# Turning x raw, scaling by channel before and by token after the products, and keeping the turned x as the residual

## The chip, the cores and the metric

The kernel runs on one core of one Trainium2 chip. A core has a matrix engine (TensorE, PE in the profile; its weight loads are PEld), a vector engine (VectorE, DVE), a scalar engine (ScalarE, ACT), a general one (GpSimd, POOL), and a queue engine (SyncE, SP) which issues most transfers. Transfers run on 16 DMA engines. Each engine works through its own list of instructions in order, and waits on semaphores. The metric is the device time of one execution in microseconds (us).

## The reference, cut to what matters

One layer of a hybrid decoder over 1024 prompt tokens and 8 x 4 sample tokens (T = 1056), 1024 channels. The part that the change touches:

```python
def rmsnorm(x, g):
    y = x * lax.rsqrt(jnp.mean(x * x, axis=-1, keepdims=True) + EPS)
    return y * g

z = rmsnorm(x, g_mix) @ w_in          # 1024 -> 5648 columns, cut into
# mLSTM q, k, v, output gate; mi, mf (4 each); FoX q, k, v (8 heads x 64); ff (8); ga, gb (1024 each)
m_ig, m_lf = mi + b_mi, log_sigmoid(mf + b_mf)
f_lf       = log_sigmoid(ff + b_ff)
y_m = mlstm(...)                      # 4 heads of 128, chunks of 128, with a state
y_f = softmax(q k^T + F[t] - F[s]) v  # FoX: 8 heads, F = cumsum(f_lf); samples over a paged cache
hm  = rmsnorm(y_m, g_mh) * sigmoid(mo)
x   = x + (sigmoid(ga) * (hm @ w_pa) + sigmoid(gb) * (y_f @ w_pb)) @ w_out
gu  = rmsnorm(x, g_ffn) @ w_gu;  x = x + (silu(gu[:F]) * gu[F:]) @ w_down     # F = 2816
x   = x + sigmoid(rmsnorm(x, g_ple) @ w_ple_gate) * (p @ w_ple_proj)
```

The factor of rmsnorm is a product of a token factor (1/sqrt of the mean square) and a channel factor (g_mix).

## The kernel before, in words

All products are in fp32 of a reduced format, in three passes: an operand is split into a high part (made by ACT) and a low part (the difference, made by DVE or POOL), and high x high, high x low and low x high are summed. The order of every engine's work is written out by hand, and there are five phases; at the end of each, all five engines wait for one another (`end_phase`, `begin_phase`).

Phase 1 (0 to 228.7 us) normalises x, turns it, and makes the first 27 units of z. A token tile of 128 rows (the ninth has the 32 sample rows) is loaded by SP, squared and summed on ACT, scaled on DVE (`norm`), turned by 8 transposes on PE (L2034), copied as the high part `acth` by ACT (L1129), and DVE makes the low part `actl` (L1547). Then PE makes the small gates mi, mf, ff for all tokens (L2050), and 27 units, each one token tile by 512 columns in 24 matmuls (L2066); the weights come in pieces of 128 x 1024 (`wraw`), of which ACT makes the high part (L1146) and POOL the low part (L927). ACT evacuates a unit to `stage` (L1153) and SP stores it to a DRAM scratch. DVE and ACT turn the gates into the running sums that later phases need; PE turns those into columns (L2072), and starts phase 2's units with `f_unit(0)` (L2089).

Phase 2 (to 447.1) has the mLSTM heads and the other 27 units.

Phase 3 (to 866.8) has the 8 FoX heads. Beside them PE makes 60 gate units, 20 blocks c = u//3 of 128 gate channels by 1056 tokens (mo, ga, gb), half a unit at a time between the steps of a head (L2220). Weights for a block: load `fraw` (`load_gate`, L744), high part on ACT (L1271), low part on POOL (`split_gate`, L988). ACT evacuates a unit to `fout` (L1278), and SP stores a block (`store_gate`, L748). A head g needs the row `nF` of its negated running sums on all partitions (`load_row`, L738), which DVE adds to the logits (L1719); `nb` (L1723) is what frees a logits bank and is awaited by PE's later logits (L2177). The head's output is divided on DVE (`yb`, L1737) and stored by SP (`store_y`, L752) when the next head is under way; DVE overwrites `yb` only after that. SP's list in phase 3 is this:

```python
for g in range(HF):
    for u in range(PRE + 7 * g if g else 0, PRE + 7 * g + 7):
        if u % 3 == 2:
            store_gate(u // 3)
            if u // 3 + 3 < NGATE // 3: load_gate(u // 3 + 3)
        if u == PRE + 7 * g + 4 and g: store_y(g - 1)
    if g < HF - 1: load_row(g + 1)
```

POOL's list has, for head g, the low part of the values (`low_values`, L984), the splits for u from PRE + 7g - 2 to PRE + 7g + 4, and the scaling of the next head's q and k (`norm_head`). PRE is 4.

Phase 4 (to 978.9) has the sample attention, in two groups of 4 sequences: keys (`keys4`, turning pages at L2286), logits, and values (`values4`, L2342). Between group 0's logits and values PE turns raw x, loaded again by SP, into `XR`, the residual with channels on partitions; `load_values(0)` (L811) waits until x is turned, since the pages lie where x was.

Phase 5 merges the branches, adds into XR, and makes the FFN and the last gate (L2396 are its matmuls). Its gate blocks are loaded from scratch (`gs`) and passed through a sigmoid on ACT (L1433), and DVE multiplies a product by them (L1914).

Of the kernel before, what the change touches and what calls it, by code (L numbers as in the profile page):

```python
# [14 lines left out]
F32 = mybir.dt.float32  # L15
# [7 lines left out]
P = 128  # L23
# [11 lines left out]
W = 512  # L35
# [19 lines left out]
def program(nc, a, o):  # L55

    ctx = ExitStack()
    with ctx:
# [42 lines left out]
        ptb = take("ptb", [1, DB * PAGES], I32)  # L101
        attn_consts_end = top[0]
# [15 lines left out]
        xt = take("xt", [P, 2, D])  # L118
        xn = take("xn", [P, 2, D])
        gmix = take("gmix", [P, D])  # L120
        ssq = take("ssq", [P, 4])
        wg = take("wg", [P, KC, GW])
        wgh = take("wgh", [P, KC, GW], F32R)
        wgl = take("wgl", [P, KC, GW], F32R)
        p1_small = top[0]
        top[0] = rows_base
        gx = take("gx", [GW, T])
# [9 lines left out]
        top[0] = max(top[0], p1_small)  # L137
        gbias = take("gbias", [GW, 1])
# [4 lines left out]
        ms_row = take("ms_row", [HM, T])  # L143
        assert top[0] <= ring_end
# [61 lines left out]
        nF = take("nF", [P, SEQ])  # L206
        qst = take("qst", [P, SEQ], F32R)
# [22 lines left out]
        xr4 = at("xr4", top[0] - GB * PAGES * W * 4, [P, NCH, D])  # L230
# [19 lines left out]
        xs4 = at("xs4", scr4, [NS, D])  # L250
# [106 lines left out]
        x_in = [sem("x_in0"), sem("x_in1")]  # L357
        small_in = sem("small_in")
        ssum_done = sem("ssum_done")
        sq_done = sem("sq_done")  # L360
        xn_done = sem("xn_done")
        xt_done = sem("xt_done")
        xhi_done = sem("xhi_done")
        xlo_done = sem("xlo_done")
        dve_own = sem("dve_own")
# [46 lines left out]
        gmh_in = sem("gmh_in")  # L412
        ecol_set = sem("ecol_set")
# [27 lines left out]
        nF_in = sem("nF_in")  # L441
        sq3 = sem("sq3")
# [50 lines left out]
        x4_in = [sem(f"x4_in{i}") for i in range(3)]  # L493
        x4_mm = sem("x4_mm")
        x4_a = sem("x4_a")
        x4_d = sem("x4_d")


# [11 lines left out]
        gv_in = again("gv_in")  # L510
        y5_in = [again("y5_in0"), again("y5_in1")]
# [78 lines left out]

        def zA_at(q, i):
            return zA_rows[q * T + i * P:q * T + i * P + trows(i), :]
# [10 lines left out]
        def _(sp):  # L603

            sp.dma_start(gmix[:], a["g_mix"][0].partition_broadcast(P)).then_inc(small_in, 16)
            sp.dma_start(ptb[:], a["page_table"].rearrange("b n -> (b n)").unsqueeze(0)).then_inc(pt_in, 16)
            sp.wait_ge(consts, 1)
            sp.dma_start(gbias[0:HM, :], a["b_mi"].rearrange("a h -> h a"), allow_slow_non_contiguous=True).then_inc(small_in, 16)
# [3 lines left out]
            w_v = a["w_in"][0].rearrange("(k p) n -> p k n", p=P)  # L612
            for c, n, src in ((0, HM, OFF_MI), (32, HM, OFF_MI + HM), (64, HF, OFF_FF)):
                sp.dma_start(wg[:, :, c:c + n], w_v[:, :, src:src + n], allow_slow_non_contiguous=True).then_inc(wg_in, 16)
            with sp.Fori(0, NCH // 2) as g:
                for s in range(2):
                    row = sp.snap(g * 256 + s * P)
                    sp.wait_ge(xn_done, 2 * g + s + 1)
                    sp.dma_start(xt[:, s], a["x_prompt"][0][bass.ds(row, P), :]).then_inc(x_in[s], 16)
            sp.wait_ge(xn_done, NCH + 1)  # L620
            sp.dma_start(xt[0:NS, 0], a["x_sample"].rearrange("b s d -> (b s) d")).then_inc(x_in[0], 16)

            def load_group(q):
                c = group_columns(q)
                for j in range(PIECES):
                    sp.wait_ge(w_lo1, q * PIECES + j + 1)
                    sp.dma_start(wraw[:, j], w_v[:, 2 * j:2 * j + 2, c:c + W]).then_inc(w_in1[j], 16)

            def store_units(q):
                for i in range(XTILES):  # L630
                    u = q * XTILES + i
# [1906 lines left out]
```

## Time and profile before

| what | value |
|---|---|
| median of 3 runs | 2133.38 us (2132.53 to 2136.48) |
| the profiled execution | 2136.39 us, of which the span is 2134.7 |
| PE, PEld busy | 91%, 85% of the span |
| DVE, ACT, POOL busy | 38%, 25%, 30% |
| mean granted clock of PE | 0.954 of full speed |
| phases end at | 228.7, 447.1, 866.8, 978.9, 2134.7 us |

The time is the device time of an execution; the span is what the profiler saw from its first to its last instruction. Shares of busy time are averages over the five phases, which have different limits: PE was busy 185.4 of phase 1's 228.7 us, 386.4 of phase 3's 419.7, and 64.2 of phase 4's 112.1.

### The profile page before, as it was taken

The page shows a single profiled execution, that of the slowest core. Times are in us where ns is not written, and L with a number is a line of the kernel's source. Part 1 is how long each engine was busy: PE and PEld are TensorE (multiplying, and loading weights), DVE is VectorE, ACT ScalarE, POOL GpSimd, SP SyncE. Part 2 cuts the span into 40 slices and gives each one's busy share as a digit, 9 for nine tenths or more (in the row PEclk, how much of TensorE's full clock was granted, in tenths as well). Part 3 has the DMA queues.
Part 4 walks back from the last instruction along what each step waited for, and adds up shares of the span by engine and source line. Part 5 has one row for each costly group of instructions (what it writes and reads, how often), then busy time and mean ns, then how long its engine had stood idle before and what let it go on. Part 6 is the DMA issues. An engine that isn't in the chain of part 4 may idle for free.

```text
span 2134.7 us, 31432 instructions
## 1 busy us (share of the span) xinstructions
PE 1936.5 (91%) x12117; PEld 1811.3 (85%) x12117; DVE 818.2 (38%) x1486; ACT 542.5 (25%) x930; POOL 642.6 (30%) x473
## 2 busy tenths in 40 slices
PE   2999999979998989465979899999999999999898
PEld 2777788868998989444979899999999999998798
DVE  4500233226655655422563232233323332235333
ACT  5311234224444543112322211001100011003311
POOL 0414223032222222002225634334333434335121
PEclk8999999989999999777999899999999999999899
DMA  4222543153323231565321211111111111120111
GB/s 126 70 87 83 172 158 117 67 156 98 95 76 99 76 95 41 181 237 209 106 90 49 69 40 39 43 55 49 49 39 39 59 39 39 41 83 25 36 56 41
DMA packets 203277, 177.78 MB, mean 83 GB/s; under 512 B 49046, under 2 KB 168058, under 8 KB 203162
## 3 DMA queue, kind: packets, MB, share of 16 engines
q1 hardware_dynamic: 156890, 159.92, 23.6%
q10 hardware_dynamic: 45280, 16.58, 3.2%
q8 instruction: 57, 0.93, 0.2%
q0 software_dynamic: 1024, 0.13, 0.1%
q14 instruction: 26, 0.21, 0.0%
HBM read 139.52 MB, written 39.24 MB: 84 GB/s over the span
## 4 chain that ended last, share of the span: by engine, by line
PE 81%; DVE 7%; issue 3%; ACT 3%; DMA 2%; SPq 2%; POOL 1%; ACTq 0%; DVEq 0%; POOLq 0%
PE pair L2396 26%; PE bank L2396 21%; PE bank L2089 7%; PE bank L2220 7%; PE bank L2066 5%; PE pair L2204 3%; PE pair L2066 2%; PE pair L2188 1%; PE pair L2286 1%; DMA scratch_yT<-yb 1%; DVE yb L1737 1%; PE pair L2177 1%; PE pair L2166 1%; SPq L796 1%; PE pair L2050 1%
## 5 line engine op out<-in xcount | busy, mean ns | idle before, releaser
L2396 PE MATMUL bank<-acth,wha 128*128 128x352 f32 x640 | 212.4, 332 | 31.6 <-DVE actl L1889 16.8
L2396 PE MATMUL bank<-actl,wha 128*128 128x352 f32 x640 | 209.6, 328 | 0.0
L2396 PE MATMUL bank<-acth,wla 128*128 128x352 f32 x640 | 209.1, 327 | 0.0
L2220 PE MATMUL bank<-acth,fwh 128*128 128x352 f32 x480 | 162.0, 337 | 15.5 <-POOL fwl L988 15.5
L2396 PE MATMUL pair<-hh,whb 128*128 128x352 f32 x528 | 171.1, 324 | 0.2 <-DVE XR L1994 0.2
L2396 PE MATMUL pair<-hl,whb 128*128 128x352 f32 x528 | 169.2, 320 | 0.0
L2396 PE MATMUL pair<-hh,wlb 128*128 128x352 f32 x528 | 169.0, 320 | 0.0
L1994 DVE TENSOR_TENSOR XR<-XR,pair 128x352 f32<-128x352 f32 x264 | 135.1, 518 | 86.0 <-PE pair L2396 84.8
L1070 POOL TENSOR_TENSOR hl<-un,hh 128x352 fp32r<-128x352 f32 x66 | 62.3, 944 | 342.6 <-ACT hh L1486 342.6
L2220 PE MATMUL bank<-acth,fwl 128*128 128x352 f32 x480 | 155.6, 324 | 0.0
L2220 PE MATMUL bank<-actl,fwh 128*128 128x352 f32 x480 | 155.1, 323 | 0.0
L2396 PEld LDWEIGHTS bank<-acth,wha 128*128 128x128 f32 x640 | 124.0, 194 | 33.8 <-DVE actl L1889 17.0
L1027 POOL CAST wha<-raw 128x1024 fp32r<-128x1024 f32 x46 | 48.9, 1064 | 329.7 <-PE pair L2396 139.8
L2089 PE MATMUL bank<-ring,acth 128*128 128x512 f32 (+1 forms) x432 | 136.6, 397 | 0.3 <-issue 0.3
L1486 ACT CAST hh<-un 128x352 fp32r<-128x352 f32 x66 | 32.2, 487 | 397.3 <-DVE un L1979 397.3
L2396 PEld LDWEIGHTS bank<-actl,wha 128*128 128x128 f32 x640 | 124.2, 194 | 0.0
L2396 PEld LDWEIGHTS bank<-acth,wla 128*128 128x128 f32 x640 | 123.8, 193 | 0.0
L1029 POOL TENSOR_TENSOR wla<-raw,wha 128x1024 fp32r<-128x1024 f32 x46 | 112.7, 2450 | 3.7
L2396 PE MATMUL pair<-acth,whb 128*128 128x352 f32 x352 | 113.5, 322 | 0.0
L2396 PE MATMUL pair<-actl,whb 128*128 128x352 f32 x352 | 112.7, 320 | 0.0
L2396 PE MATMUL pair<-acth,wlb 128*128 128x352 f32 x352 | 112.7, 320 | 0.0
L1029 POOL TENSOR_TENSOR wlb<-raw,whb 128x1024 fp32r<-128x1024 f32 x44 | 105.6, 2399 | 3.5
(442 smaller groups left out, 4803.5 us busy)
## 6 DMA issues: line engine op xcount, KB each, us to landing
raw<-in_w_gu SPq DMA_DIRECT2D x44, 512.0 KB, 3.8
wraw<-in_w_in SPq DMA_DIRECT2D x24, 512.0 KB, 5.8
scratch_zA<-stage SPq DMA_DIRECT2D x48, 256.0 KB, 2.0
raw<-in_w_down SPq DMA_DIRECT2D x22, 512.0 KB, 3.6
scratch_zT<-fout SPq DMA_DIRECT2D x20, 528.0 KB, 3.1
fraw<-in_w_in SPq DMA_DIRECT2D x20, 512.0 KB, 4.9
gs<-scratch_zT SPq DMA_DIRECT2D x16, 528.0 KB, 3.5
kpg<-in_cache_k SPq DMA_DIRECT2D x32, 256.0 KB, 5.2
```

Of the source, the lines that this page charges most:

```text
L796: return [sp.value_load(ptb[0:1, n:n + 1], min_val=0, max_val=NPOOL - 1) for n in range(g * GB * PAGES, (g + 1) * GB * PAGES)]
L1027: nc.gpsimd.tensor_copy(hi, raw[:, j]).then_inc(pool_own, 1)
L1029: nc.gpsimd.tensor_tensor(lo, raw[:, j], hi.bitcast(F32), ALU.subtract).then_inc(w_split, 1)
L1070: nc.gpsimd.tensor_tensor(hl[:, j, t * TW:(t + 1) * TW], un[:, (3 * j + t) % 2, :], hh[:, j, t * TW:(t + 1) * TW].bitcast(F32), ALU.subtra ...
L1486: nc.scalar.copy(hh[:, j, t * TW:(t + 1) * TW], un[:, v % 2, :]).then_inc(h_hi, 1)
L1737: own.step(nc.vector.reciprocal(y, pC[DH:, m * 256:(m + 1) * 256]))
L1994: nc.vector.tensor_tensor(x, x, BANK[4 + u % 4][:, 0:TW], ALU.add).then_inc(x6_done, 1)
L2066: ins = nc.tensor.matmul(BANK[u % 3][0:rows, :], x[:, k, i * P:i * P + rows], w, start=n == 0, stop=n == 3 * KC - 1)
L2089: ins = nc.tensor.matmul(BANK[u % 2][0:rows, :], x[:, k, i * P:i * P + rows], w, start=n == 0, stop=n == 3 * KC - 1)
L2204: ins = nc.tensor.matmul(pC[:, m * 256 + skip:(m + 1) * 256], v[:, j, :], x[:, base + j * 256 + skip:base + (j + 1) * 256], start=n == 0, ...
L2220: ins = nc.tensor.matmul(BANK[u % 2][:, 0:TW], w[:, c % 2, k, :], x[:, k, t * TW:(t + 1) * TW], start=n == 0, stop=n == 3 * KC - 1)
L2396: ins = nc.tensor.matmul(out, w[i](k), x[j](k), start=n == 0, stop=n == total - 1)
```

## The change

- Phase 1: x is not normalised ahead. A tile is turned raw; DVE multiplies it by g_mix, a factor per partition now (`tile_scaled`, from `gcol`), which gives `tf`; ACT copies the raw turned tile for a store to a scratch `xT`, and makes the high part of `tf`; DVE makes the low part. The squares are summed meanwhile, and the token factor `rstd` comes in two lots. The unit of a tile follows its turn, and ACT multiplies by `rstd` as it evacuates a unit, here and in phase 2. The small gates come behind the first nine units; for them, `rstd` is put in a row on all partitions (`rvB`) by 9 matmuls with diagonals. x and the first weights are first in SP's list.
- Phase 3: that row, stored and loaded as `rv3`, multiplies each gate block in `fout` on POOL (`scale_gate`, a multiply of 128 x 1056), and `store_gate` waits for this.
- Phase 4: the loads, transposes and copies of x go, with their waits.
- Phase 5: SP loads `XR` from `xT` in 9 transfers behind `hst5`, 4.33 MB, and DVE waits for them before w_out's loop.

```diff
+            load_tile(0)
+            load_piece0(0, 0)
+            load_piece0(0, 1)
+            load_tile(1)
+            load_piece0(0, 2)
+            load_piece0(0, 3)
+            load_tile(2)
             sp.dma_start(ptb[:], a["page_table"].rearrange("b n -> (b n)").unsqueeze(0)).then_inc(pt_in, 16)
             sp.wait_ge(consts, 1)
+            for c, n, src in ((0, HM, OFF_MI), (32, HM, OFF_MI + HM), (64, HF, OFF_FF)):
+                sp.dma_start(wg[:, :, c:c + n], w_v[:, :, src:src + n], allow_slow_non_contiguous=True).then_inc(wg_in, 16)
+            for i in range(XTILES):
+                store_tile(i)
+                if i + 3 < XTILES:
+                    load_tile(i + 3)
+                if 2 <= i < 6:
+                    load_piece0(1, i - 2)
+                if i >= 3:
+                    store_unit(i - 3)
...
+            sp.dma_start(RS[2 * HM:2 * HM + 1, :], rvB[0:1, :]).then_inc(rows_out, 16)
...
             def store_gate(c):
-                sp.wait_ge(f_out, 3 * c + 3)
+                sp.wait_ge(f_rv, c + 1)
                 sp.dma_start(o["zT"][c * P:(c + 1) * P, :], fout[:, c % 2, :]).then_inc(f_st[c % 2], 16)
...
             load_row(0)
+            sp.dma_start(rv3[:], o["rows"][2 * HM:2 * HM + 1, :].partition_broadcast(P).rearrange("p a t -> p (a t)")).then_inc(g_in, 16)
             sp.dma_start(gqk[:, 0, :], a["g_qn"][0].partition_broadcast(P)).then_inc(g_in, 16)
...
             def load_values(g, pages):
-                sp.wait_ge(x4_mm, XTILES)
                 if g:
                     sp.wait_ge(o4_mm, g)
...
             pages = load_pages(0)
             load_keys(0, pages)
-            sp.wait_ge(ms4, 1)
-            sp.dma_start(xs4[:], a["x_sample"].rearrange("b s d -> (b s) d")).then_inc(x4_in[0], 16)
-            for i in range(2):
-                sp.dma_start(xr4[:, 4 * i:4 * i + 4, :], a["x_prompt"][0][512 * i:512 * i + 512, :].rearrange("(i p) d -> p i d", p=P)).then_inc(x4_in[1 + i], 16)
             load_values(0, pages)
...
             sp.dma_start(hst5[:], o["hT"].rearrange("(c p) t -> p c t", p=P)).then_inc(h5_in, 16)
+            for i in range(XTILES):
+                sp.dma_start(XR[:, :, token_cols(i)], xT_at(i)).then_inc(xr_in, 16)
             for c in range(2, KC):
                 if c % 2 == 0 and c < 6:
...
+            def scale_gate(c):
+                pool.wait_ge(f_out, 3 * c + 3)
+                nc.gpsimd.tensor_tensor(fout[:, c % 2, :], fout[:, c % 2, :], rv3[:], ALU.mult).then_inc(f_rv, 1)
+
             def split_gate(c):
                 pool.wait_ge(f_hi, c + 1)
                 nc.gpsimd.tensor_tensor(fwl[:, c % 2], fraw[:, c % 2], fwh[:, c % 2].bitcast(F32), ALU.subtract).then_inc(f_lo, 1)
...
             pool.wait_ge(g_done, 1)
+            pool.wait_ge(g_in, 48)
             norm_head(0)
             for g in range(HF):
                 low_values(g)
                 for u in range(PRE + 7 * g - 2 if g else 0, PRE + 7 * g + 5):
-                    if u % 3 == 2 and u // 3 + 2 < NGATE // 3:
-                        split_gate(u // 3 + 2)
+                    if u % 3 == 2:
+                        if u // 3 + 2 < NGATE // 3:
+                            split_gate(u // 3 + 2)
+                        scale_gate(u // 3)
                 if g < HF - 1:
                     norm_head(g + 1)
+            for u in range(PRE + 7 * HF - 2, NGATE):
+                if u % 3 == 2:
+                    scale_gate(u // 3)
             end_phase(pool)
 
...
+            def tile_out(i):
+                act.wait_ge(tf_done, i + 1)
+                if i >= 2:
+                    act.wait_ge(xs_st[i % 2], 16 * (i // 2))
+                nc.scalar.copy(xs[:, i % 2, :, 0:trows(i)], turn_pair(i)).then_inc(xs_done, 1)
+                nc.scalar.copy(acth[:, :, token_cols(i)], tf[:, i % 2, :, 0:trows(i)]).then_inc(xhi_done, 1)
...
+                if u == 0 or u == 4:
+                    act.wait_ge(rs_done, u // 4 + 1)
+                nc.scalar.mul(stage[0:rows, u % 3], unit_bank(u)[0:rows, :], rstd[0:rows, u % XTILES:u % XTILES + 1]).then_inc(unit_out, 1)
...
-                nc.scalar.copy(stage[0:rows, u % 3], BANK[u % 2][0:rows, :]).then_inc(fu_out, 1)
+                i = u % XTILES
+                nc.scalar.mul(stage[0:rows, u % 3], BANK[u % 2][0:rows, :], rstd[0:rows, i:i + 1]).then_inc(fu_out, 1)
...
+            def tile_scaled(i):
+                if i == 0:
+                    dve.wait_ge(g_col, 16)
+                dve.wait_ge(xt_done, i + 1)
+                if i >= 2:
+                    dve.wait_ge(xlo_done, i - 1)
+                nc.vector.tensor_tensor(tf[:, i % 2, :, 0:trows(i)], turn_pair(i), gcol[:].unsqueeze(2).to_broadcast([P, KC, trows(i)]),
+                                        ALU.mult).then_inc(tf_done, 1)
+
+            def tile_low(i):
+                dve.wait_ge(xhi_done, i + 1)
+                nc.vector.tensor_tensor(actl[:, :, token_cols(i)], tf[:, i % 2, :, 0:trows(i)], acth[:, :, token_cols(i)].bitcast(F32),
+                                        ALU.subtract).then_inc(xlo_done, 1)
...
+                nc.vector.reciprocal(rstd[:, first:last], ssq[:, first:last]).then_inc(rs_done, 1)
+
+            tile_scaled(0)
+            for i in range(1, XTILES):
+                if i == 3:
+                    recips(0, 0, 4)
+                if i == 7:
+                    recips(1, 4, XTILES)
+                tile_scaled(i)
+                tile_low(i - 1)
+            tile_low(NCH)
+            dve.wait_ge(rs_done, 2)
+            dve.wait_ge(xlo_done, XTILES)
+            for i in range(XTILES):
+                n = trows(i)
+                ins = nc.vector.tensor_scalar(dg[0:n, i, 0:n], ident[0:n, 0:n], rstd[0:n, i:i + 1], None, ALU.mult)
+            ins.then_inc(dg_done, 1)
             dve.wait_ge(gate_mm, 1)
+            nc.vector.tensor_copy(rvB[:, 0:512], BANK[5][:])
+            nc.vector.tensor_copy(rvB[:, 512:SEQ], BANK[7][:])
+            nc.vector.tensor_copy(rvB[:, SEQ:], BANK[4][:, 0:NS]).then_inc(dg_done, 1)
+            dve.wait_ge(dg_done, 2)
...
             for t in range(NT):
-                ins = nc.vector.tensor_scalar(gx[:, t * TW:(t + 1) * TW], BANK[5 + t][0:GW, 0:TW], gbias[:, 0:1], None, ALU.add)
+                cols = slice(t * TW, (t + 1) * TW)
+                own.step(nc.vector.tensor_tensor(gx[:, cols], BANK[2 + t][0:GW, 0:TW], rvB[0:GW, cols], ALU.mult))
+                ins = nc.vector.tensor_scalar(gx[:, cols], gx[:, cols], gbias[:, 0:1], None, ALU.add)
             ins.then_inc(gate_x, 1)
+            dve.wait_ge(gate_x, 1)
             dve.wait_ge(gate_l, 1)
...
+            dve.wait_ge(xr_in, 16 * XTILES)
...
+            def turn_tile(i):
+                pe.wait_ge(x_in[i % 3], 16 * (i // 3) + 16)
+                if i >= 2:
+                    pe.wait_ge(xs_done, i - 1)
+                n = trows(i)
                 for k in range(KC):
-                    ins = nc.tensor.transpose(BANK[2 * s + k // 4][:, (k % 4) * P:(k % 4) * P + rows],
-                                              xn[0:rows, s, k * P:(k + 1) * P], ident[0:rows, 0:rows])
+                    ins = nc.tensor.transpose(PAIR[i % 2][:, k * P:k * P + n], xt[0:n, i % 3, k * P:(k + 1) * P], ident[0:n, 0:n])
                 ins.then_inc(xt_done, 1)
...
+            turn_tile(0)
+            turn_tile(1)
+            for i in range(XTILES):
+                if i + 2 < XTILES:
+                    turn_tile(i + 2)
+                unit(i)
+
+            pe.wait_ge(dg_done, 1)
+            for i in range(XTILES):
+                n = trows(i)
+                out = BANK[5 + i // 4 * 2][:, i % 4 * P:(i % 4 + 1) * P] if i < NCH else BANK[4][:, 0:NS]
+                ins = nc.tensor.matmul(out, ones[0:n, :], dg[0:n, i, 0:n], start=True, stop=True)
+            ins.then_inc(gate_mm, 1)
+            pe.wait_ge(wg_lo, 1)
+            for t in range(NT):
+                n = 0
...
+                if t == 2:
+                    pe.wait_ge(dg_done, 2)
...
             pe.wait_ge(unit_out, MG * XTILES)
+            pe.wait_ge(col_done, 1)
             f_unit(0)
...
-            for n in range(XTILES):
-                i = (n - 1) % XTILES
-                if n in (0, 1, 5):
-                    pe.wait_ge(x4_in[(n + 3) // 4], 16)
-                if n >= 2:
-                    pe.wait_ge((x4_a, x4_d)[n % 2], n // 2)
-                for k in range(KC):
-                    x = xr4[:, i, k * P:(k + 1) * P] if i < NCH else xs4[:, k * P:(k + 1) * P]
-                    ins = nc.tensor.transpose((pA, pB)[n % 2][:, k * P:k * P + trows(i)], x, ident[0:trows(i), 0:trows(i)])
-                ins.then_inc(x4_mm, 1)
             values4(0)
-            pe.wait_ge(x4_a, 5)
-            pe.wait_ge(x4_d, 4)
             keys4(1)
```

Not shown: buffers, semaphores, the rest of the fixed order of ACT in phase 1 (per slot a square, `tile_out`, a weight piece, `unit_evac`), and w_in's later groups in SP's list.

## Rows read from the trace of the kernel before

**Rows 1.** The page, part 4: the chain that ended last, by engine.
```profile
PE 81%; DVE 7%; issue 3%; ACT 3%; DMA 2%; SPq 2%; POOL 1%; ACTq 0%; DVEq 0%; POOLq 0%
```

**Rows 2.** Chain of waits, phase 1: start us, length us, what.
```profile
5.25 4.02 DMA xt<-in_x_prompt
...
58.67 14.10 PE pair L2050 x72
72.78 11.13 PE bank L2066 x48
...
224.07 16.93 PE bank L2089 x72
```

**Rows 3.** Groups by line and form, ACT and POOL, phases 1 and 3.
```profile
L1146 ACT CAST wh<-wraw 128x1024 fp32r<-128x1024 f32 x8 | 8.1, 1053 | 6.3 <-DMA wraw<-in_w_in 6.3
...
L927 POOL TENSOR_TENSOR wl<-wraw,wh 128x1024 fp32r<-128x1024 f32 x8 | 18.9, 2393 | 32.1 <-ACT wh L1146 32.1
...
L988 POOL TENSOR_TENSOR fwl<-fraw,fwh 128x1024 fp32r<-128x1024 f32 x20 | 47.7, 2385 | 114.1 <-ACT fwh L1271 113.9
```

**Rows 4.** Instructions of DVE in time: start us, us, what.
```profile
225.05 0.27 DVE L1604 COPY col<-pair 32x128 f32<-32x128 f32 x1
...
568.92 1.23 DVE L1747 TENSOR_TENSOR klo<-pair,khh 128x1024 fp32r<-128x1024 f32 x1
```

**Rows 5.** PE's waits in phase 3; chain in head 1; clock in head 3.
```profile
PE pair L2177 <- DVE nb L1723: 15.0, 4, 6.8
...
540.23 6.18 DMA scratch_yT<-yb
...
550.04 0.50 PE pair L2177
...
648.00:654.00 6.00, 5.02 (x20) 4.32 (x21) 5.42 (x16) 4.99 (x7) 0.04 (x1) 0.50 0.00 0
```

**Rows 6.** Instructions of POOL in heads 1 and 2.
```profile
523.84 2.39 POOL L988 TENSOR_TENSOR fwl<-fraw,fwh 128x1024 fp32r<-128x1024 f32 x1 [1.50 <-ACT fwh L1271]
540.37 2.40 POOL L988 TENSOR_TENSOR fwl<-fraw,fwh 128x1024 fp32r<-128x1024 f32 x1 [14.13 <-ACT fwh L1271]
...
568.74 1.30 POOL L984 TENSOR_TENSOR vl<-v,vh 128x512 fp32r<-128x512 f32 x1 [6.56 <-ACT vh L1319]
569.99 2.37 POOL L988 TENSOR_TENSOR fwl<-fraw,fwh 128x1024 fp32r<-128x1024 f32 x1
```

**Rows 7.** SP's issues around head 2; tile nF: time from issue to landing.
```profile
539.37 0.34 SPq L748 DMA_DIRECT2D scratch_zT<-fout  x1
...
561.39 0.34 SPq L748 DMA_DIRECT2D scratch_zT<-fout  x1
...
562.25 1.04 SPq L738 DMA_DIRECT2D nF<-scratch_rows  x1
...
DMA to landing us min/median/max: 3.6/5.6/7.3
```

**Rows 8.** Instructions of DVE and PE in heads 1 and 2.
```profile
524.27 1.98 DVE L1723 SCALAR_TENSOR_TENSOR nb<-mx,fcol 128x1 f32<-128x1 f32 x1
...
570.91 0.29 DVE L1719 CUSTOM_DVE_ANT_0 lg<-pair,nF 128x128 f32<-128x128 f32 x1
...
572.90 0.34 PE L2177 MATMUL pair<-khh,qst 128*128 128x384 f32 x1
```

**Rows 9.** SP's issues in phase 4.
```profile
918.83 8.16 SPq L811 DMA_DIRECT2D vpg<-in_cache_v  x16
```

**Rows 10.** Chain of waits, phase 4.
```profile
908.55 0.72 ACT px L1388
...
942.25 6.39 PE pair L2286 x32
...
962.68 0.72 ACT px L1388
...
967.23 5.84 PE bank L2342 x32
```

**Rows 11.** Start of phase 5: stretches (DMA share, GB/s last), ACT, chain.
```profile
979.00:1005.00 26.00, 12.83 (x70) 12.83 (x71) 8.32 (x9) 11.56 (x11) 7.92 (x4) 0.68 0.98 354
...
1008.94 1.09 ACT L1433 ACTIVATE gs<-gs 128x1056 f32<-128x1056 f32 x1 [5.33 <-DMA gs<-scratch_zT]
...
1013.14 3.82 PE pair L2396 x24
```

More of the change, by code:

```diff
@@ L124, in program @@
         wgl = take("wgl", [P, KC, GW], F32R)
+        gcol = take("gcol", [P, KC])
+        ssq = take("ssq", [P, NCH + 1])
         p1_small = top[0]
         top[0] = rows_base
+        rvB = take("rvB", [P, T])
         gx = take("gx", [GW, T])
@@ L206, in program @@
         nF = take("nF", [P, SEQ])
+        rv3 = take("rv3", [P, T])
         qst = take("qst", [P, SEQ], F32R)
@@ L611, in _ @@
             sp.dma_start(sm[:], a["state_m"][0].rearrange("b h -> h b"), allow_slow_non_contiguous=True).then_inc(small_in, 16)
[L612 to L631, printed above, removed]
[L632 to L638 removed]
+            for u in range(6, XTILES):
+                store_unit(u)
+            for j in range(PIECES):
+                load_piece0(2, j)
             sp.wait_ge(rows_done, 1)
@@ L1126, in high_parts @@
-            def high_parts(s, rows, n, c0):
-                act.wait_ge(xt_done, n + 3)
-                for b in range(2):
-                    nc.scalar.copy(acth[:, 4 * b:4 * b + 4, bass.ds(c0, rows)],
-                                   BANK[2 * s + b][:, :].rearrange("p (k t) -> p k t", k=4)[:, :, 0:rows]).then_inc(xhi_done, 1)
-            with act.Fori(0, NCH // 2) as g:
-                for s in range(2):
-                    squares(s, P, 2 * g + s, g + 1)
-                for s in range(2):
-                    high_parts(s, P, 2 * g + s, act.snap(g * 256 + s * P))
@@ L1137, in _ @@
-            squares(0, NS, NCH, NCH // 2 + 1)
-            high_parts(0, NS, NCH, SEQ)
-            act.wait_ge(wg_in, 48)
-            nc.scalar.copy(wgh[:], wg[:]).then_inc(wg_hi, 1)
-            def split_group(q):
-                for j in range(PIECES):
-                    act.wait_ge(w_in1[j], 16 * (q + 1))
-                    nc.scalar.copy(piece_parts(q, j)[0], wraw[:, j]).then_inc(w_hi1, 1)
+            act.dma_start(gcol[:], a["g_mix"][0].rearrange("(k p) -> p k", p=P), allow_slow_non_contiguous=True).then_inc(g_col, 16)
@@ L1148, in unit_evac, with roots, high_piece @@
+            def roots(first, last):
+                act.wait_ge(ssum_done, last)
+                nc.scalar.activation(ssq[:, first:last], ssq[:, first:last], ACT.Sqrt, scale=1.0 / D, bias=epsc[:, 0:1]).then_inc(sq_done, 1)
+            def high_piece(q, j):
+                act.wait_ge(w_in1[j], 16 * (q + 1))
+                nc.scalar.copy(piece_parts(q, j)[0], wraw[:, j]).then_inc(w_hi1, 1)
             def unit_evac(u):
@@ L1414, in _ @@
             attend(0)
-            for n in range(0, XTILES, 2):
-                residual_tile(n)
             store_out(0)
```

240 lines of the change are left out of this document (133 added, 107 removed).

## The prediction, on record before the change was run

> **What bounds the kernel now.** I read the page first, then the chain of waits phase by phase, then the single queues of phase 3. The chain line gives PE 81% of the span [rows 1]: whatever PE doesn't wait for is free, and each microsecond it stands costs one. So the question for every edit is whether PE's next instruction comes earlier or later. There are four places. In phase 1 the first long PE run is the gates at 58.67; before it PE only has transposes, in a chain of x landing, square, root, scale and turn that is walked nine times, and from the gates to f_unit(0) at 224.07 PE is full [rows 2]. In phase 3 PE is nearly full, and the waits of logits for nb are 15.0 us in four places [rows 5]. In phase 4 values(0) and keys(1) wait for pages that are loaded late [rows 9, 10]. At the start of phase 5 the DMA engines are busy 98% of the time [rows 11].
>
> The sum is made against the profiled execution (2136.39 us: span 2134.7 and 1.7 around it), which is 3.0 above the median 2133.38; I take the 3.0 off at the end.
>
> **Phase 1 (gain).** Removed: normalising before the turn, four rounds of ACT root and DVE scale between load and PE. Added: 9 DVE multiplies by g_mix, 9 ACT copies of the raw turned tile, 9 stores, 9 diagonals and 9 small matmuls for the row rvB, 3 DVE copies of it, one more multiply per gate block. x is first in SP's queue instead of behind seven other loads: today its transfer starts at 5.25 and takes 4.02 [rows 2], so it lands near 5. Turn of tile 0 ends at 6.9. The multiply from PSUM is priced at the 1.23 of a DVE subtraction of 128x1024 from PSUM [rows 4]; ACT meanwhile makes two high weight pieces at 1.05 each [rows 3], then two copies of the tile, DVE the low part: unit 0 starts near 14.7. It then needs the low parts of pieces 2 and 3, which POOL makes at 2.39 each, one behind the other [rows 3], to about 22; unit 0 ends at 24.5. From there PE is full: 8 units of 5.565 (two are 11.13 [rows 2]) and 6 turns of 1.0 give 75.0; diagonals 1.0; the gates, 72 matmuls of 352 columns against the unit's 24 of 512, 5.565 x 3 x 352/512 = 11.5, to 87.5 (14.10 today [rows 2], partly at the low clock); 18 units, 100.2, to 187.7; turning of the columns 1.0, and f_unit(0) now waits for DVE's copies of them, the last of which ends at 225.32 [rows 4], some 1.3 behind f_unit(0)'s start of today. So f_unit(0) starts at 190.0 instead of 224.07: **-34**. ACT has some 5 us of work in each slot of 6.6 (a square, two copies and a weight piece at about 1.05 each by [rows 3], the evacuation half of that) and hides there; without that cover a slot would grow to ACT's. Bounds: -22 if the first weights and the 4-byte pieces of gcol land as late as x lands today, with ACT's slots the longer; -38 if pieces 2 and 3 don't hold unit 0. I take the worked value.
>
> **Phase 2 and start of phase 3.** The evacuation by a multiply instead of a copy has the same form. The row rv3 is one more issue in SP's tail before phase 3 begins for all engines; a row of this kind takes 1.04 to issue [rows 7]. Bounds 0.5 and 1.1; I take **+0.8**.
>
> **Phase 3, the y store (loss).** store_gate(c) no longer follows fout's evacuation but POOL's scale, and POOL does the scale behind split_gate(c+2). SP takes its list in order, so store_y(g-1), queued behind store_gate, waits too. In head 1: split 540.37 to 542.77 [rows 6], then the scale of 128x1056, priced as split's 2.39 x 1056/1024 = 2.46 [rows 3], so the store goes at 545.3 instead of 539.37, 5.9 later. Behind it stands the y store; its landing (540.23 plus 6.18) releases yb, then nb and PE's logits(7) at 550.04 [rows 5]. PE already waits there in heads 1, 3, 4 and 6 (the four waits of [rows 5]), so the delay goes straight to PE: 4 x 5.9 = 23.6. In heads 2 and 5 the y store follows a block store with a gap, so it goes only 0.6 later, but then beside two other transfers, which I put at 3 more for its landing, less 1.0 of slack: 2.2 and 2.0, estimates; head 7 some 0.7. **+28.5**, bounds 23 and 31.
>
> **Phase 3, the row nF (loss).** SP's list has load_row(g+1) at the end of head g. For u = 17, 23, 38 and 44 the store_gate before it belongs to head g for SP, but POOL's list takes that scale in head g+1, behind low_values(g+1) and a split. In head 2 low_values begins at 568.74 and split ends at 572.36 [rows 6], the scale at 574.9; the row, today 0.86 behind the store's issue and issued at 562.25 [rows 7], is issued at 575.8. It lands 3.6 to 7.3 later, median 5.6 [rows 7]; with the 7.3 that head 2 has today, 583.1. DVE's first bias, today at 570.91 [rows 8], needs it; nb(0) follows 0.6 later, and PE's logits(2), today at 572.90 [rows 8], wait for nb(0): a stall of 10.8. The same working in head 3 (split behind low_values again, row issued at 621.6) and in heads 5 and 6 gives 9.1, 9.8 and 9.2. **+39** in four heads; with every landing at 3.6 it is 32, at 7.3 it is 44.
>
> **The clock behind these stalls.** After the 6.6 us wait of head 3 the granted clock was 0.50 from 648 to 654, with PE 5.02 us busy [rows 5]: that is the 1.2 GHz level, and half of the time is lost, some 2.4. Six of the new stalls are as long (four of nF, and heads 1 and 4 whose y wait was short before): **+14**, bounds 0 and 15.
>
> **POOL's port.** A DVE nb of usually 0.22 took 1.98 at 524.27 and ended with POOL's split that ran from 523.84 [rows 8, 6]; 20 scales are 20 more POOL stretches of 2.46. Nearly all fall where nb has slack or would meet the split anyhow: I take **+2**, bounds 0 and 40. The Trainium skill speaks against the change here: SBUF — State Buffer, in SBUF: two separate sides, has VectorE with two SBUF inputs and GpSimd take the shared port in turn, and the loser blocks for the whole instruction. The trace agrees for that nb (1.98 against 0.22); by that rule alone, with every scale meeting an nb on the path, the sum would be some 40 higher, which is rival 4.
>
> **Phase 4 (gain).** The turning of x for the residual goes, with its 4.3 MB of loads, and the values' pages no longer wait for it (issued from 918.83 on [rows 9]). In group 1 the first value matmul starts 4.55 behind the exponent (962.68 to 967.23 [rows 10]); the exponent of group 0 is at 908.55 [rows 10] and no longer held by x, so values(0) would start at 913.1 and take about the 6.9 of group 1 (5.84 and 1.0 for the sums), to 920. keys(1) starts near 920.9 instead of 942.25 [rows 10]: **-21.5**. Bounds: -15 if the pages of group 1, whose loads move up, are late by as much as they are awaited today; -24.
>
> **Phase 5 (loss).** 4.33 MB of XR are loaded ahead of the gates and of w_pb's last pieces, in a stretch where the DMA engines are 98% busy at 354 GB/s [rows 11]: 4.33 MB at 354 to 405 GB/s are 10.7 to 12.2. ACT gets its third gate block at 1008.94, after a wait of 5.33 [rows 11]; then near 1020, and PE, which needs the bank that DVE frees with it (unit 10 at 1013.14 [rows 11]), stands 8.5 and some 2 for the clock. **+10.5**, bounds 4 (half of XR passes beside) and 14.
>
> **Sum:** -34 + 0.8 + 28.5 + 39 + 14 + 2 - 21.5 + 10.5 = +39 us, so 2175.5 in the profiled execution and **2172** on the median's basis. The single bounds, taken together as independent, make 2157 to 2190 the likeliest case's own range.
>
> **Rivals.**
> 1. Faster: the late store in phase 3 is hidden (SP has slack, or POOL catches up before PE needs nF and yb). Then the gains of phases 1 and 4 remain less phase 5: -34 - 21.5 + 10.5 + 0.8 = -44, 2089. For it: in the other four heads nF lands long before the bias. Against it: yb is awaited already in four heads, and nF's store order follows from the two lists.
> 2. Only the nF half holds, the y store being hidden: -44 + 39 + 10 = +5, 2138. Only the y half (nF prefetched in time): -44 + 28.5 + 5 = -11, 2122. Against both: the same scale stands ahead of both.
> 3. Phase 1 doesn't come out: ACT or the first transfers become its bound. The point is a slot of ACT over 6.6 us; at 7.5 the gain falls by 8, and with weights 10 later to some -15: 2190.
> 4. Slower on the port: every scale meets an nb, and the 2.46 goes to PE in most of the 20 blocks: +40 instead of +2, 2210. It decides if nb's mean in phase 3 rises above 1 us.
>
> **How the numbers follow.** Forecast 0.64; rival 1 0.08; rival 2 0.13 (0.08 nF only, 0.05 y only); rival 3 0.08; rival 4 0.07. Faster than 0.2% below the median (4.3 us, about what a measurement of this kernel tells from no change) are rival 1, y only, and a small part of nF only: 0.15. Within 0.2%: 0.04, out of nF only. Slower: 0.81. The range 2136 to 2198 takes in the terms' bounds, rival 3 and most of nF only, and leaves out rivals 1 and 4.
>
> **What would show it.** f_unit(0) near 190 (phase 1). In the SP queue the rows of nF in heads 2, 3, 5 and 6 issued behind the scale, some 7 us after low_values begins, and PE's logits waiting for nb for about 10 us four times; waits for the y store of 6 to 13 in heads 1, 3, 4 and 6, with the granted clock at 0.50 behind them. keys(1) some 21 earlier within phase 4. In phase 5 a wait of DVE for the third gate block near 10. It is wrong if nF lands before the bias is due, or if the scales are done before low_values of the next head.

## The result, and the profile after

The changed kernel takes 2190.22 us (median of 4 runs, 2188.74 to 2195.2) against 2133.9 before: a ratio of 1.0267, 95% interval 1.0251 to 1.0283. The forecast was 2172, slower, with a range of 2136 to 2198; the way and the range hold, the size is 18 us short. The profiled executions differ by 53.4 us (a span of 2187.9 against 2134.7). By phase, with the begin of each read from the first instruction behind `begin_phase`:

| stretch | before | after | difference | forecast |
|---|---|---|---|---|
| phases 1 and 2 | 447.1 | 425.6 | -21.5 | -33.2 |
| phase 3 | 419.7 | 504.4 | +84.7 | +83.5 |
| phase 4 | 112.1 | 87.4 | -24.7 | -21.5 |
| phase 5 | 1155.8 | 1170.5 | +14.7 | +10.5 |
| sum | 2134.7 | 2187.9 | +53.2 | +39 |

First the page's chain line, to be held against [rows 1]:

```profile
PE 75%; DVE 7%; DMA 5%; issue 4%; POOL 4%; SPq 3%; ACT 3%; DVEq 0%; ACTq 0%; POOLq 0%
```

PE lost six points of the chain to DMA and POOL: PE now waits for transfers, and these for POOL's instructions. Where, the waits of PE in phase 3 say (engine, line, what it waited for: us, times, longest), against the 15.0 us in four places of [rows 5]:

```profile
PE pair L2280 <- DVE nb L1812: 77.5, 12, 12.4
...
PE pair L2307 <- DVE ptl L1817: 11.1, 14, 4.3
```

`lg` are a head's logits, to which DVE adds nF and of which ACT takes the exponent, with `nb` as its bias; PE turns the outcome, ACT makes its high part `pth`, and DVE its low part `ptl`.

The start of head 2, which answers to [rows 6 to 8]: four views, one behind the other: POOL's instructions, SP's issues, the landing of nF on the chain of waits, and the PE instruction that waited (in brackets the idle time before it):

```profile
559.91 1.30 POOL L1022 TENSOR_TENSOR vl<-v,vh 128x512 fp32r<-128x512 f32 x1 [8.23 <-ACT vh L1400]
561.16 2.39 POOL L1030 TENSOR_TENSOR fwl<-fraw,fwh 128x1024 fp32r<-128x1024 f32 x1
563.50 2.44 POOL L1026 TENSOR_TENSOR fout<-fout,rv 128x1056 f32<-128x1056 f32 x1
```
```profile
565.96 0.34 SPq L786 DMA_DIRECT2D scratch_zT<-fout  x1
566.34 0.43 SPq L782 DMA_DIRECT2D fraw<-in_w_in  x1
566.82 1.02 SPq L776 DMA_DIRECT2D nF<-scratch_rows  x1
```
```profile
566.82 5.59 DMA nF<-scratch_rows
```
```profile
573.31 0.69 PE L2280 MATMUL pair<-khh,qst 128*128 128x384 f32 x1 [9.08 <-DVE nb L1812]
```

The row of F is issued 6.9 us behind the begin of low_values instead of 6.5 ahead of it, and PE stands 9.08 us. Before that, in head 1, the y store's chain, against [rows 5, 6]:

```profile
525.02 2.40 POOL fwl L1030
527.42 2.46 POOL fout L1026
529.89 0.34 SPq L786
530.27 0.43 SPq L782
530.75 5.13 DMA scratch_yT<-yb
```

Split, scale, block store, weights' load and only then the y store. Phase 1 has a wait that the forecast didn't have. Chain of waits, SP's issues, and PE's waits:

```profile
1.90 10.38 DMA gcol<-in_g_mix
...
201.21 16.94 PE bank L2191 x72
```
```profile
121.28 0.28 SPq L674 DMA_DIRECT2D scratch_rows<-lfm  x1
...
123.21 8.17 SPq L642 DMA_DIRECT2D scratch_zA<-stage  x6
```
```profile
PE bank L2139 <- ACT stage L1193: 6.9, 1, 6.9
```

SP waits until 121.28 for the gates' rows, and behind them in its list stand the stores of units 9 and on. `stage` has three buffers, and so has PE for its units: PE's unit 15 stood 6.9 us for an evacuation, which stood for a store. f_unit(0) starts at 201.21, not at the 190 of the forecast (224.07 before, [rows 2]). In phase 5 PE's wait, SP's issues and ACT's third gate block, against [rows 11]:

```profile
PE pair L2485 <- DVE tpart L2000: 12.5, 1, 12.5
```
```profile
1030.32 25.40 SPq L888 DMA_DIRECT2D XR<-scratch_xT  x9
```
```profile
1063.51 1.08 ACT L1503 ACTIVATE gs<-gs 128x1056 f32<-128x1056 f32 x1 [20.78 <-DMA gs<-scratch_zT]
```

### The profile page after: what moved, and what is told of

Read it like the earlier page. It is cut to its first block, busy times and chain, and to the rows that moved or that the text cites. A ratio compares the mean times of both kernels' runs of the same rounds, so it can differ in the third digit from the quotient of the medians.

```text
span 2187.9 us, 31227 instructions
## 1 busy us (share of the span) xinstructions
PE 1940.7 (89%) x12063; PEld 1812.7 (83%) x12063; DVE 808.3 (37%) x1481; ACT 541.3 (25%) x912; POOL 687.6 (31%) x494
## 3 DMA queue, kind: packets, MB, share of 16 engines
q1 hardware_dynamic: 167340, 164.26, 23.8%
## 4 chain that ended last, share of the span: by engine, by line
PE 75%; DVE 7%; DMA 5%; issue 4%; POOL 4%; SPq 3%; ACT 3%; DVEq 0%; ACTq 0%; POOLq 0%
PE pair L2485 26%; PE bank L2485 20%; PE bank L2191 7%; PE bank L2323 6%; PE bank L2139 3%; PE pair L2307 2%; PE pair L2139 2%; DMA scratch_yT<-yb 2%; POOL fout L1026 1%; POOL fwl L1030 1%; SPq L888 1%; PE pair L2291 1%; DMA nF<-scratch_rows 1%; DVE yb L1826 1%; PE pair L2280 1%
## 5 line engine op out<-in xcount | busy, mean ns | idle before, releaser
L2323 PEld LDWEIGHTS bank<-acth,fwh 128*128 128x128 f32 x480 | 94.1, 196 | 17.1 <-issue 17.1
```

The costliest lines, as they stand in the source:

```text
L2323: ins = nc.tensor.matmul(BANK[u % 2][:, 0:TW], w[:, c % 2, k, :], x[:, k, t * TW:(t + 1) * TW], start=n == 0, stop=n == 3 * KC - 1)
```

## The experiments

The theory is that of the forecast, the queue theory: the price of the change is not its work, but that SP's list is in order, and that entries which others need stand behind one that now waits longer. Its rival is the port theory (rival 4): 20 multiplies on POOL hold up DVE and POOL themselves. Times are medians beside the kernel before on the same chip (2133.7 to 2135.0).

**The row ahead of the late store.**

```diff
                     if u % 3 == 2:
+                        if u >= PRE + 7 * g + 5 and g < HF - 1:
+                            load_row(g + 1)
                         store_gate(u // 3)
...
-                if g < HF - 1:
+                if g < HF - 1 and (PRE + 7 * g + 6) % 3 != 2 and (PRE + 7 * g + 5) % 3 != 2:
                     load_row(g + 1)
```

> SP's list alone: where the last store of a head waits for a scale of the next head (heads 2, 3, 5, 6), the load of nF now stands ahead of that store. Queue theory (the cost is what stands behind the late store in SP's list): the four waits of logits(2) for nb(0), 9.1, 8.8, 8.9 and 9.1 us, go, and with them the low clock behind each (2.4), so phase 3 falls from 504.3 to about 458 and the time from 2190 to about 2145. Port theory (the 20 multiplies themselves hold up DVE and POOL): POOL's work is the same, so phase 3 moves by under 10 and the time stays above 2180.

2157.58 us, ratio 1.0103 (1.0075 to 1.0131); phase 3 took 473.9. PE's waits in it:

```profile
PE pair L2282 <- DVE nb L1814: 41.6, 8, 12.4
PE pair L2309 <- DVE ptl L1819: 17.4, 16, 4.3
```

The waits for nb fell by 35.9, just the four of nF (9.1, 8.8, 8.9, 9.1), but the time by 33 instead of 45: the weights' load is still behind the late store, and ACT's copy of these weights stands ahead of `pth` in ACT's list. PE's waits for ptl rose from 11.1 to 17.4. The next entry of the same queue took over part of the cost. The rest of the missing 12 is not the queue's: PE's waits for ACT's exponent rose from 0.9 to 5.3 us (the meetings of nb with a scale, see the run without scales and with late stores), and PE's busy time fell by 5.4 and not by the four times 2.4 expected of the clock.

**The y store ahead of the block store.**

```diff
                     if u % 3 == 2:
+                        if u in (PRE + 7 * g + 3, PRE + 7 * g + 4) and g:
+                            store_y(g - 1)
                         store_gate(u // 3)
...
-                    if u == PRE + 7 * g + 4 and g:
+                    if u == PRE + 7 * g + 4 and u % 3 == 1 and g:
                         store_y(g - 1)
```

> SP's list alone: in heads 1, 3, 4, 6 and 7 the store of the last head's y stands ahead of the gate block's store. Queue theory: the waits of logits(7) for nb, 6.0, 12.4, 6.2 and 12.4 us, go altogether, those that the kernel before had among them, and the low clock behind them: phase 3 from 504.3 to about 460, the time from 2190 to about 2146. Port theory: under 10 us.

2144.19 us, 1.0048 (1.0033 to 1.0063); phase 3 took 459.1, as the queue theory said. The waits for nb fell by 36.7, to:

```profile
PE pair L2282 <- DVE nb L1814: 40.8, 9, 9.1
```

**All block stores late.**

```diff
-                    if u % 3 == 2:
-                        store_gate(u // 3)
-                        if u // 3 + 3 < NGATE // 3:
-                            load_gate(u // 3 + 3)
+                    if u % 3 == 2 and u // 3 + 3 < NGATE // 3:
+                        load_gate(u // 3 + 3)
                     if u == PRE + 7 * g + 4 and g:
                         store_y(g - 1)
+                    if u % 3 == 1 and u >= 4:
+                        store_gate(u // 3 - 1)
...
+            store_gate(NGATE // 3 - 1)
```

> SP's list alone: the next weights' load comes first, then y, and each gate block's store two units later, so that nothing stands behind a scale. The scales stay where they are. Queue theory: all eight long waits and the late weights of head 0 (6.5 us) go, and the clock stays up: phase 3 at 405 to 415, below the 419.7 of the kernel before, and 2093 to 2103 in all. Port theory: phase 3 stays above 460, the time above 2145.

2097.26 us, 0.9825 (0.9801 to 0.9848); phase 3 took 412.3, both as the queue theory said. Nothing but SP's order differs from the changed kernel, and 93 us are gone. PE's waits for nb:

```profile
PE pair L2281 <- DVE nb L1813: 1.5, 3, 0.5
```

**No scaling.** The two calls of `scale_gate` are left out, and `store_gate` waits for `f_out` as before.

> Leaves out the scaling of the gate blocks (they lack the token factor), and the store follows fout's evacuation as before; the rest of the change stands. Both theories: phase 3 back at the 419.7 of the kernel before, give or take 3, the time near 2105. Queue theory: that is 5 to 15 above the run with late stores, which has the scales and lacks the old waits for y. Port theory: 40 or more below the run with late stores.

2102.15 us, 0.9843 (0.9816 to 0.9871); phase 3 took 419.5, the 419.7 of the kernel before. Both theories had this; what parts them is that it is 5 above the run that has the scales and late stores, where the port theory wanted 40 or more below: that theory falls as an account of the 84.7 us.

**Units ahead of the rows, phase 1.** SP's rows of the gates go behind the stores of units 9 to 14.

```diff
-            sp.wait_ge(rows_done, 1)
-            ...
-            for u in range(XTILES, 2 * XTILES):
+            for u in range(XTILES, XTILES + 6):
+                store_unit(u)
+            sp.wait_ge(rows_done, 1)
+            ...
+            for u in range(XTILES + 6, 2 * XTILES):
                 store_unit(u)
```

> SP's list in phase 1 alone: the stores of units 9 to 14 stand ahead of the rows of the gates, for which SP waits until 121.3. Queue theory: PE's wait of 6.95 us at 122.9 (no stage buffer is free, since the stores stand behind the rows) goes, with some 2 us of the low clock: f_unit(0) at about 192 instead of 201.2, the time from 2190 to about 2181. Rival (ACT is held up by the gates' chain of Abs, Exp and Ln itself): PE still waits for an evacuation, f_unit(0) after 199, the time above 2187.

2182.62 us, 7.6 less; phases 1 and 2 took 417.0 instead of 425.6, and the 6.9 us for `stage` are no longer among PE's waits. f_unit(0) starts at 192.9, near the 192 of the queue theory; the rival wanted it after 199.

**XR late, in a lump.** The nine loads stand ahead of w_out's weights instead of ahead of the gate blocks.

> SP's list in phase 5 alone: the nine loads of XR go behind all gate blocks and w_pa's pieces, just ahead of w_out's. Queue theory: SP is no longer held for 25 us ahead of the gate blocks, PE's wait of 12.5 us for the third gate block goes with 2 us of low clock: phase 5 from 1170.5 to 1156, the time to about 2176. Rival (the 4.3 MB cost transfer time wherever they stand): PE waits about 10 us before or at w_out's loop instead, the time above 2185.

2186.76 us, only 3.5 less; phase 5 took 1164.1. That is the rival's figure. But the trace has a queue in it again: SP's issue of the nine took 14.95 us, with w_out's weights behind it (SP's issues, then PE's waits). In both places the lump held what follows, so this run alone doesn't tell the two apart; the one with XR spread does.

```profile
1131.21 14.95 SPq L904 DMA_DIRECT2D XR<-scratch_xT  x9
```
```profile
PE bank L2485 <- POOL wla L1077: 20.6, 2, 17.5
```

**The three orders together.**

> The three changes of SP's order together: block stores late, units ahead of the rows, XR late. No arithmetic differs from the changed kernel. Queue theory: 2097.3 less 9 and less 14, so 2074, 2.8% below the kernel before. Rival (the waits share a cause, and one takes the place of another): 2085 or more.

2079.18 us, 0.9741 (0.9725 to 0.9757). Phases: 416.4, 411.7, 86.9 and 1162.2. The 5 above the expected 2074 lie in phase 5, 1162.2 against the 1156 expected: XR's lump.

**No scaling, and block stores late.** The scale is left out of the third run.

> Leaves out the scaling of the gate blocks (they lack the token factor) and has the block stores late, so that neither a scale nor a queued entry costs anything in phase 3. With the late stores and the scales phase 3 took 412.3. If the scales cost nothing but their place in the list: 411 to 413 here. If POOL's port costs something: about 400 to 405 (419.5 less the old waits for y of 6.7 and 6.8 and the low clock of 2.4 behind each), and the time near 2087; what is left, 8 to 12 us, is the price of 20 multiplies on POOL.

2088.76 us, from two executions 6.2 us apart; phase 3 of the profiled one took 402.0 against 412.3. So 20 scales cost 10.3 us in this pair of traces, once nothing hides them (the medians differ by 8.5). Where: DVE's second nb in head 2 and POOL's scale beside it, and then that nb in the run without scales:

```profile
551.84 2.04 DVE L1813 SCALAR_TENSOR_TENSOR nb<-mx,fcol 128x1 f32<-128x1 f32 x1
```
```profile
551.39 2.47 POOL L1027 TENSOR_TENSOR fout<-fout,rv 128x1056 f32<-128x1056 f32 x1
```
```profile
548.49 0.22 DVE L1809 SCALAR_TENSOR_TENSOR nb<-mx,fcol 128x1 f32<-128x1 f32 x1
```

The nb that meets the scale takes 2.04 and ends at 553.88, two hundredths behind the scale's 553.86; alone it takes 0.22. The rule of the Trainium skill (SBUF — State Buffer, SBUF: two separate sides) that one of the two blocks for the other's whole instruction agrees with this pair. In the run with late stores each of the 21 nb over 1 us ends within 0.03 us of a split or scale that it met, but only six of the 20 scales are met by one, once each in heads 0, 2, 3, 5, 6 and 7.

Of the 10.3 us, 7.1 are idle time of PE (33.8 against 26.7) and 3.1 its busy time, at a granted clock of 0.984 against 0.988. PE's waits for nb are 1.5 in both: it waits further down the chain, for ACT's exponent in heads 0, 2, 3, 5 and 6 (first view; none without scales) and for ptl (9.8 against 8.2). The chain of head 2 (second view) shows that the meeting is not all of it:

```profile
PE pair L2292 <- ACT lg L1380: 5.5, 5, 1.2
```
```profile
551.84 2.05 DVE nb L1813
...
555.04 2.43 ACTq L1389
...
559.42 0.91 PE pair L2308 x6
```

Behind the late exponent in ACT's list stand the issues of the next head's q, k and v, of which v's takes 2.43 us, and behind those the copy `pth`. Without scales v's issue takes 2.19 at the same place and isn't on the chain. So an entry in ACT's list takes part in this price too; no run parts the two.

**g_mix turned, XR spread, and both.** On the three orders: g_mix is loaded as 8 rows of 512 bytes and turned by PE; and/or the XR loads stand two by two behind the gate blocks from the fourth on.

```diff
-            act.dma_start(gcol[:], a["g_mix"][0].rearrange("(k p) -> p k", p=P), ...).then_inc(g_col, 16)
+            act.dma_start(grow[:], a["g_mix"][0].rearrange("(k p) -> k p", p=P)).then_inc(g_col, 16)
...
                 load_gates(c % 2, (12 + c) * P)
+                for i in range(2 * c - 6, 2 * c - 4):
+                    if 0 <= i < XTILES:
+                        sp.dma_start(XR[:, :, token_cols(i)], xT_at(i)).then_inc(xr_in, 16)
```

> The run with all three orders, and g_mix loaded as 8 rows of 512 bytes and turned by PE, in place of 1024 pieces of 4 bytes that landed at 12.3. If the landing of gcol sets unit 0 (tf at 12.3, then tile_out, then the weight pieces 2 and 3): tile 0 is scaled near 7 to 8 and f_unit(0) comes 3 to 4 us earlier, 2075 to 2076. Rival (the weights' pieces, which share the DMA engines, set unit 0): within 1.5 of 2079.

> As the run with all three orders, but the loads of XR stand two by two behind the gate blocks from the fourth on, in the stretch where the queue is idle, instead of in one lump ahead of w_out's weights. Queue theory (any nine loads in a lump hold SP and what is behind): PE's wait of 17.0 us for w_out's pieces goes, the old waits there (2.9 and 9.2) come back, phase 5 from 1162.2 to 1156, 2073. Rival (4.3 MB cost 10 us of PE wherever they are): no gain, 2079 or above.

> Both of the last two. If they are independent: the gains add, 2069 to 2070.

2085.19, 2078.58 and 2071.93 us (2079.4 to 2086.8, 2074.0 to 2080.8, 2067.5 to 2080.4). The totals bear out none of the gains expected: g_mix alone is slower than both of its figures, the spread alone stands at its rival's, and both together miss by 2. By phases the spread does what the queue theory expected, and the 4.3 MB cost PE nothing: phase 5 took 1154.9 and 1155.4 in the two runs that have it, 1162.2 and 1162.1 in those that don't, 1155.8 in the kernel before. g_mix is worth 1.3 to 2.5 in phases 1 and 2 (414.4 against 415.7, 413.9 against 416.4), between the two expectations: PE then waits for the weights' low parts. That is little more than traces differ by: the seven with phases 1 and 2 as in the changed kernel lie between 425.5 and 427.1. What hides both in the totals is phase 3, which none of the edits touches: 420.6, 419.3 and 413.5 (see the last section).

**POOL's scale ahead of low_values.** On both of the last: in heads 2, 3, 5 and 6 POOL does the scale that SP's list counts to the head before while it would stand idle.

```diff
+                first = PRE + 7 * g - 2 if g else 0
+                early = [u for u in range(first, first + 2) if g and u % 3 == 2]
+                for u in early:
+                    scale_gate(u // 3)
                 low_values(g)
...
-                        scale_gate(u // 3)
+                        if u not in early:
+                            scale_gate(u // 3)
```

> As the run with XR spread and g_mix turned, but POOL does the scales of u = 17, 23, 38 and 44 ahead of low_values of the next head, where it stood idle for some 7 us, instead of behind low_values and a split. If the 10 us that the multiplies still cost in phase 3 come from the meeting of a scale with the second nb of a head (1.98 to 2.04 us instead of 0.22, in heads 2, 3, 5 and 6): phase 3 falls from 413.5 by 4 x 2 to about 405, and the time to 2063 to 2066. Rival (the cost is that of 20 multiplies wherever they stand): phase 3 stays at 411 or above, the time at 2070 or above.

2066.25 us (2065.37 to 2067.79), 0.9678 (0.9665 to 0.9691), phase 3 at 406.9, between the 405 expected and the rival's 411, and 6.6 less than in the run before it. POOL and DVE at the start of head 2:

```profile
530.46 2.45 POOL L1032 TENSOR_TENSOR fout<-fout,rv 128x1056 f32<-128x1056 f32 x1
537.67 1.29 POOL L1028 TENSOR_TENSOR vl<-v,vh 128x512 fp32r<-128x512 f32 x1 [4.77 <-ACT vh L1411]
538.92 2.38 POOL L1036 TENSOR_TENSOR fwl<-fraw,fwh 128x1024 fp32r<-128x1024 f32 x1
```
```profile
541.71 0.22 DVE L1825 SCALAR_TENSOR_TENSOR nb<-mx,fcol 128x1 f32<-128x1 f32 x1
```

The scale begins 7.2 us ahead of low_values and ends 4.8 ahead of it, and the second nb takes 0.22. This version beats the kernel before by 3.2%, with the change's arithmetic whole.

## Why the prediction was right

The way, the range and the mechanism came out as forecast; the size was 18 us short. Of these, 14 are terms (+39 forecast, +53.2 measured): 11.7 in phases 1 and 2, 1.2 in phase 3, 4.2 in phase 5, less 3.2 in phase 4. The other 4 are the basis: 3.0 was taken off for the kernel before, whose profiled execution lay that far above its median, while that of the changed kernel lay 0.5 below.

**Phase 1, -34 forecast, -22.9 measured** (f_unit(0) at 201.2, start of phase 3 21.5 earlier). This is the term that was mis-sized. About its lower bound, -22, came, but not for the bound's reason (late first weights, ACT's slots). The start was about right (unit 0 ended near 26 instead of 24.5, held by gcol, which landed at 12.3; with g_mix turned, it ended at 23.8 and 24.4). The failing step is the last: "18 units, 100.2, to 187.7". I followed ACT's and PE's lists through the gates, but not SP's, where the stores of the units stand behind the wait for the gates' rows. The run with the units ahead gives 8.6 us of the missing 11 back. It is the mechanism that I charged to phase 3, in the phase where I didn't look for it.

**Phase 2 and the row rv3, +0.8 forecast, +1.4 measured**, past the bound of 1.1 (22.9 earlier at f_unit(0), 21.5 at phase 3).

**The y store, +28.5 forecast, +26.6 measured**: 77.5 less nF's 35.9 less the 15.0 of before. The waits in heads 1, 3, 4 and 6 are 6.0, 12.4, 6.2 and 12.4. One detail of the working was wrong: the fourth of the old waits, 0.5, was in head 0 and not in head 4, where PE now waits 6.2 all the same. The terms of heads 2, 5 and 7 (2.2, 2.0 and 0.7) came as 2.3, 1.0 and 0.8; the 3 us put there for the transfers beside the y store came from no row.

**The row nF, +39 forecast, +35.9 measured**: 9.1, 8.8, 8.9 and 9.1 against 10.8, 9.1, 9.8 and 9.2. The row landed in 5.59 in head 2 and not in the 7.3 that it took before. The lower bound of 32 was added up wrongly: with the landings of the four heads before (7.3, 5.6, 6.4 and 5.7) all put at 3.6, the same working gives 28.

**The clock, +14 forecast, some +16**: PE's busy time in phase 3 is the same 2592 matmuls before and after, and grew from 386.43 to 402.74 in the stretches of the two traces (before, then after; behind the comma PE's busy time, and third from the end the granted clock, 0.97 and 0.90):

```profile
447.10:866.80 419.70, 386.43 (x2592) 367.63 (x2592) 239.16 (x465) 183.45 (x280) 115.39 (x78) 0.97 0.31 86
425.60:930.00 504.40, 402.74 (x2592) 379.86 (x2592) 240.34 (x465) 184.40 (x280) 163.69 (x98) 0.90 0.26 72
```

**Head 0, nothing forecast, +6.2 measured** (head 1's low_values begins 80.1 us into phase 3 instead of 73.9; some 2 of it are the low clock, counted above): the weights' load behind the first late store (chain of waits):

```profile
454.96 2.44 POOL fout L1026
457.41 0.36 SPq L786
...
457.82 6.61 DMA fraw<-in_w_in
464.48 0.92 issue
465.40 0.37 ACT pth L1383
465.80 0.44 DVE ptl L1817
466.24 0.04 issue
466.28 1.54 PE pair L2307 x6
```

The working took fraw's load as hidden; in head 0 the scale waits behind low_values, which starts at 451.3, and ACT's copy of the weights holds `pth`. The miss and the smaller terms of y, nF and the port nearly cancel: that phase 3 came out within 1.2 is luck in part, since its terms were off by 2 to 4 each. Phase 3 adds up from PE's waits and work: nb +62.5, ptl +5.0 (11.1 against 6.1), the first weights +1.3, the clock +16.3, together 85.1 for a difference of 84.7.

**The port, +2 forecast.** In the changed kernel as it stands, next to nothing shows: nb's mean in phase 3 went from 558 to 577 ns, since DVE stood waiting for nF while POOL scaled; rival 4, which wanted nb above 1 us, falls. With the queue mended it is 10.3, ACT's entry included. Had the forecast been for the mended order, this term would have been the wrong one.

**Phase 4, -21.5 forecast, -24.7 measured**, a little past the bound of -24: keys(1) began 21.1 us earlier within the phase, as forecast, and the other 3.6 lie behind its begin (the granted clock was 0.57 in its first 6.5 us before, and 1.00 in its first 5 us now).

**Phase 5, +10.5 forecast, +14.7 measured**: the wait was foreseen at 8.5 and was 12.5. The working charged the 4.33 MB with the DMA engines' rate; the issue of the nine loads alone held SP for 25.4 us, and the third gate block was issued only behind it; it reached ACT 16 us later in the phase, not 11. The rest is 1.4 more of PE's busy time and 1.3 more of its first wait.

Of the rivals, the first and both halves of the second fall with the runs that mend nF or y alone: each half is there, and of nearly the forecast size. The third was half right (the gain is smaller), but ACT did none of it, and the first transfers 1.5.

## What to carry to other kernels

When an instruction in an in-order list gets a later releaser, walk every list that waits for it, in every phase, and write down what stands behind it and who needs that; here that walk priced phase 3's two large terms to within 2 and 3 us; where it was left out, in phase 1, the wait that it missed cost 8.6. Before a change is judged by its time, its order is worth a second look: the same arithmetic took 2190 us and, with entries moved on SP and POOL and one load reshaped and turned by PE, 2066. A fix that moves one entry can only hand the wait to the next one behind (nF to the weights, gate blocks to w_out's weights), and nine loads in a lump held what followed in both of the places tried, while spread into an idle stretch they cost PE nothing.

## What the runs showed that was not expected

A pause of PE of the same length was followed by the low clock in one execution and not in another. In head 2, at the same place in the program, XR spread alone (first view) and XR spread with g_mix turned (second), whose phase 3 has the same instructions in the same order; stretches of 1 us, with PE's busy time behind the comma, and the granted clock third from the end:

```profile
547.00:548.00 1.00, 0.60 (x4) 0.31 (x2) 0.19 (x1) 0.16 (x1) 0.00 (x0) 1.00 1.09 263
548.00:549.00 1.00, 0.33 (x3) 0.31 (x3) 0.86 (x3) 1.00 (x4) 0.00 (x0) 1.00 1.25 288
549.00:550.00 1.00, 0.47 (x4) 0.26 (x3) 0.65 (x4) 0.85 (x2) 0.00 (x0) 1.00 1.21 290
550.00:551.00 1.00, 1.00 (x7) 1.00 (x7) 0.49 (x1) 0.47 (x2) 0.00 (x0) 0.58 1.27 263
551.00:552.00 1.00, 1.00 (x4) 1.00 (x5) 0.06 (x1) 0.00 (x0) 0.00 (x0) 0.50 1.36 218
```
```profile
546.00:547.00 1.00, 0.80 (x6) 0.51 (x4) 0.36 (x3) 0.00 (x0) 0.00 (x0) 1.00 0.83 203
547.00:548.00 1.00, 0.05 (x1) 0.05 (x1) 0.58 (x3) 0.88 (x3) 0.00 (x0) 1.00 1.27 297
548.00:549.00 1.00, 0.50 (x3) 0.26 (x3) 0.94 (x4) 0.85 (x3) 0.00 (x0) 1.00 1.21 282
549.00:550.00 1.00, 0.97 (x8) 0.97 (x9) 0.21 (x1) 0.76 (x2) 0.00 (x0) 1.00 1.26 279
```

PE idles 1.60 us in the three stretches of the first and 1.68 in the four of the second; the clock fell to 1.2 GHz only in the first. It repeats in heads 3, 5 and 6, at 1.5 to 1.6 us a head, 6.2 in all, and phase 3 of the two traces differs by 5.7 (419.3 and 413.5). What decides it stays open. With the scale ahead of low_values PE's idle time in heads 2 and 5 falls from 2.3 and 2.4 us to 0.6, in heads 3 and 6 from 3.8 to 2.1 and 3.1; the granted clock is 1.00 in all four, and the five times of that kernel agree within 2.4 us.
